# Turning gathered expert rows on TensorE: operands retyped from float32 to float32r

## The reference, cut to what matters

```python
xb = x_pad[rows]                                  # gather the rows of one expert
h = jax.nn.silu(xb @ w_gate[e]) * (xb @ w_up[e])  # 1024 -> 256
yb = (h @ w_down[e]) * rw[:, None]                # 256 -> 1024
return acc.at[rows].add(yb), None
```

## Time and profile before

| | |
|---|---|
| median of 3 runs | 1641.59 us (1641.39 to 1642.97) |
| profiled execution: span from its first to its last instruction | 1640.5 us (no time of it beside the span is given) |
| PE busy | 1578.0 us, 96% of the span |
| PE weight loads | 1310.0 us, 80% |
| DVE busy | 1182.3 us, 72% |
| ACT busy | 1032.5 us, 63% |
| POOL busy | 503.7 us, 31% |
| mean granted TensorE clock | 0.979 of full speed |

### The profile page before, as it was taken

How to read it: one execution, slowest core, us unless ns; L and a number is a source line. 1 busy time by engine, 2 the same in 40 slices (tenths; PEclk the granted TensorE clock), 3 DMA queues, 4 the chain that set the end, 5 groups by cost and what they waited for, 6 DMA issues and landing times.

```text
span 1640.5 us, 32188 instructions
## 1 busy us (share of the span) xinstructions
PE 1578.0 (96%) x8246; PEld 1310.0 (80%) x8247; DVE 1182.3 (72%) x2036; ACT 1032.5 (63%) x1706; POOL 503.7 (31%) x495
## 2 busy tenths in 40 slices
PE   6999999999999999899999999999999999999986
PEld 6897888888887788778878888888888888888863
DVE  4214777777777788847777787777876787888866
ACT  3214666666666655527677787666776777877854
POOL 0000000000000135432544454543454445454426
PEclk9999999999999999899999999999999999999995
DMA  7223222222123533657999999999999999999987
GB/s 245 91 81 91 72 48 68 58 65 71 45 71 103 170 134 138 227 196 281 337 291 318 305 357 367 326 289 264 334 318 288 274 353 331 342 368 370 367 252 282
DMA packets 161320, 368.63 MB, mean 225 GB/s; under 512 B 53009, under 2 KB 73489, under 8 KB 161265
## 3 DMA queue, kind: packets, MB, share of 16 engines
q1 hardware_dynamic: 136272, 284.21, 49.7%
q0 software_dynamic: 24992, 83.73, 19.7%
HBM read 294.39 MB, written 65.11 MB: 219 GB/s over the span
## 4 chain that ended last, share of the span: by engine, by line
PE 72%; DVE 8%; DMA 8%; issue 5%; ACT 3%; ACTq 2%; POOL 1%; SPq 0%; DVEq 0%; POOLq 0%
PE bank_pair L1025 6%; PE bank_pair L1031 6%; PE bank_pair L1028 6%; DMA sums_scratch<-ys,sidx 5%; PE q_ps L91 4%; PE q_ps L93 4%; PE q_ps L92 4%; PE out_ps L916 4%; PE k_ps L894 4%; PE out_ps L1084 3%; PE out_ps L1085 3%; PE q_ps L1015 3%; PE k_ps L1052 2%; PE k_ps L1053 2%; PE k_ps L1060 2%
## 5 line engine op out<-in xcount | busy, mean ns | idle before, releaser
L1918 DVE TENSOR_TENSOR gu_lo<-raw_gu,gu_hi 128x1024 fp32r<-128x1024 f32 x260 | 306.3, 1220 | 25.5 <-ACT gu_hi L1396 25.5
L1396 ACT CAST gu_hi<-raw_gu 128x1024 fp32r<-128x1024 f32 x260 | 253.2, 1050 | 2.3 <-DMA raw_gu<-in_moe_w_gate_dram 1.5
L1025 PE MATMUL bank_pair<-gu_hi,xb_hi 128*128 128x512 f32 x576 | 233.1, 405 | 5.5 <-DVE gu_lo L1918 4.2
L1028 PE MATMUL bank_pair<-gu_lo,xb_hi 128*128 128x512 f32 x576 | 226.9, 394 | 0.0
L682 POOL DMA_INDIRECT sums_scratch<-ys,sidx x63 | 122.1, 1939 | 148.9 <-DMA sums_scratch<-ys,sidx 116.0
L1918 DVE TENSOR_TENSOR dn_lo<-raw_dn,dn_hi 128x1024 fp32r<-128x1024 f32 x130 | 152.6, 1213 | 2.9 <-ACT dn_hi L1396 2.4
L1031 PE MATMUL bank_pair<-gu_hi,xb_lo 128*128 128x512 f32 x576 | 142.7, 390 | 2.0 <-DVE xb_lo L1922 2.0
L1301 ACT CAST pt_hi<-k_ps 128x512 fp32r<-128x512 f32 (+1 forms) x192 | 85.7, 482 | 75.4 <-PE k_ps L894 74.7
L1025 PEld LDWEIGHTS bank_pair<-gu_hi,xb_hi 128*128 128x128 f32 x576 | 110.1, 191 | 28.8 <-issue 6.4
L613 POOL IOTA e<- 128x64 f32 x1 | 0.2, 185 | 428.8 <-DVE xs L1714 428.8
L1396 ACT CAST dn_hi<-raw_dn 128x1024 fp32r<-128x1024 f32 x130 | 130.0, 1052 | 2.9 <-DMA raw_dn<-in_moe_w_down_dram 2.9
(11 more groups left out here) (306 smaller groups left out, 3973.7 us busy)
## 6 DMA issues: line engine op xcount, KB each, us to landing
raw_gu<-in_moe_w_gate_dram SPq DMA_DIRECT2D x128, 512.0 KB, 6.8
raw_gu<-in_moe_w_up_dram SPq DMA_DIRECT2D x128, 512.0 KB, 8.6
raw_dn<-in_moe_w_down_dram SPq DMA_DIRECT2D x128, 512.0 KB, 8.3
wqk<-in_fox_w_in_dram SPq DMA_DIRECT2D x66, 128.0 KB, 2.5
v_scratch<-v_out SPq DMA_DIRECT2D x32, 256.0 KB, 2.8
va<-v_scratch SPq DMA_DIRECT2D x16, 512.0 KB, 4.7
fin<-sums_scratch SPq DMA_DIRECT2D x16, 512.0 KB, 8.3
xs<-in_x_dram SPq DMA_DIRECT2D x8, 512.0 KB, 7.4
```

The lines of the kernel that those rows point to most:

```text
L1025: i = pe.matmul(o3, xb_hi[s][:, c], g_hi[:, :, c], start=c == 0, stop=False, skip_group_check=True)
L1028: pe.matmul(o3, xb_hi[s][:, c], g_lo[:, :, c], start=False, stop=False, skip_group_check=True)
L1396: a.copy(hi, raw).then_inc(S[done], 1)
L1918: dve.tensor_tensor(lo, raw, hi, ALU.subtract).then_inc(S[lo_ok], 1)
```

## The change

A second identity `identr` of type F32R is allocated (128x128, 512 bytes in each partition, ahead of all later buffers) and filled by POOL with a copy of `ident`, after the two masks. POOL and PE each get one more wait for this copy. The 8 transposes of `turn_rows` and the 8 of `turn_further` read the rows as F32R (a reinterpretation of the same bytes, with no rounding ahead of it), take `identr` as moving operand and write PSUM as F32R. The other transposes of the kernel (L794, L894, L901, L983, L1039, L1093) stay as they were.

```diff
         ident = sb("ident", [P, P])
         identb = sb("identb", [P, P], BF16)
+        identr = sb("identr", [P, P], F32R)
...
             g.affine_select(out=upto[:], in_=upto[:], compare_op=ALU.is_ge, fill=0.0, base=0,
                             pattern=[[1, T]], channel_multiplier=-1).then_inc(S["masks"], 1)
+            g.tensor_copy(identr[:], ident[:]).then_inc(S["masks"], 1)
+
+            pool.wait_ge(S["masks"], 8)
             pool.wait_ge(S["v_ps"], NVC * TT // 2)
...
             def turn_rows(src, ps):
                 v = strided(src[:, 0:D])
                 for c in range(DC):
-                    i = pe.transpose(ps[:, c * P:(c + 1) * P], v[:, c], ident[:])
+                    i = pe.transpose(ps[:, c * P:(c + 1) * P].bitcast(F32R), v[:, c].bitcast(F32R), identr[:])
                 return i
...
                 v = strided(xg[2][rows, 0:D])
                 for c in range(DC):
-                    i = pe.transpose(banks[1][:, FF + c * XR:FF + (c + 1) * XR], v[:, c], ident[rows, rows])
+                    i = pe.transpose(banks[1][:, FF + c * XR:FF + (c + 1) * XR].bitcast(F32R), v[:, c].bitcast(F32R), identr[rows, rows])
                 i.then_inc(S["x_turned"], 1)
...
+            pe.wait_ge(S["masks"], 8)
             pe.wait_ge(rows_in[0], 16)
             pe.wait_ge(S["r1_ok"], TT - 1)
             turn_rows(xg[0], q_ps).then_inc(S["turned"], 1)
```

## The result

The changed kernel takes 1651.07 us (median of 4 runs, 1649.98 to 1652.06) against 1642.28 us for the kernel before (median of 4, 1641.39 to 1643.32). The ratio is 1.0055 with an interval of 1.0042 to 1.0069: 9.0 us slower, interval 6.9 to 11.3. 1641.3 was forecast and 1645.5 was the upper end, so it is more than the range held.

The account below looks back on a forecast made before the run. PE's instruction stream in the experts was taken to bound the kernel. Span 1640.5 + 0 (loads) - 0.3 (group ends) + 0 (copy) + 0 (memory) = 1640.2, with 1.1 around it 1641.3 us; range 1635 to 1645.5.

Parts of the forecast that it names:

- The load of the rows: PE's weight loads in 824 turns: rounded strided pitch 112 ns against 111, +0.8 us, taken as 0 +-2.5 us.
- rival 2: Loads in both kinds of turn: stride and type surcharges add up, pitch 161 ns, +41 us, 1683 us; chance 0.06.
- The bounds: Rounded strided load in a turn: from 51 ns less (plain adjacent load) to about 50 ns more (stride on top of type).
- Wrong towards slower: loads of 240: Sign in the turns' weight loads: a duration of 240 ns would show the forecast wrong towards slower.
- Right: loads of 190: Sign in the first-row turns: loads still at some 190 ns, eight of them in 0.97 us, would show the forecast right.
- The ends of a group: Behind each group's last turn: `q_ps` finished about 49 ns earlier, taken as -0.3 us, bounds 0 and -3.5 us.
- The stream goes from 109 to about 60: Moving identity in first-row turns: rounded stream about 60 ns instead of 109, alone moving no start as the load takes 111.
- copy, wait and memory: Identity's POOL copy and PE's wait: cost 0, without cover 0.3 us; buffers shifted by 512 bytes: unpriced, +-1 us.
- Rule and row on the fast load: Turn loads: the skill's rule read literally makes F32R loads fast; rows say otherwise, bf16 load 97 ns, rounded 188.

Follow-up runs that it names:

- e7: Kernel before with first-row turns as ordinary rounded products with the identity, adjacent columns (low bits lost, wrong weight rows), further rows plain: 1641.51 us, one run.
- e6: Kernel before with first-row turns as ordinary rounded products with the rounded identity, same stride (low bits lost), further turns plain: 1703.71 us, ratio 1.0373.
- e4: Kernel before with first rows turned rounded from adjacent columns (wrong weight rows), further rows plain and strided: 1631.39 us, ratio 0.9929.
- e5: Kernel before with first rows turned plain from adjacent columns (wrong weight rows), further rows plain and strided: 1639.41 us, ratio 0.9989.
- b9: Kernel before with rows written in turn order by the normalisation, all turns adjacent, down weights reordered, only first rows rounded: 1627.16 us, ratio 0.9907.
- e1: Changed kernel with both kinds of turn back to plain, keeping `identr`, its copy and the waits: 1641.94 us, ratio 1.0001 to the kernel before.
- e11: Kernel before with only the further rows rounded, from adjacent columns (wrong weight rows), first rows plain and strided: 1634.91 us, one run.
- b5: Kernel before with gate and up weights loaded in adjacent-column order (1 KB runs), both kinds of turn adjacent, first rows rounded: 1642.09 us, ratio 1.0006.

## Why the prediction was wrong, step by step

- **The step that failed** is "The load of the rows", the term 824 x (112 - 111) = +0.8 us, taken as 0 +-2.5. The load's pitch is 133 and 131, so the term is 824 x 0.022 = +18 us nominally, +15.1 between the neighbouring matmuls. Both neighbours that I set around it were far in the respect that mattered: the earlier trace rows is rounded and adjacent but no turn (e7: 112, e6: 239), is a turn but plain. The agreement of 188 and 193 ns in the earlier trace rows, on which I leaned against rival 2, meant nothing for a turn: a rounded load with adjacent columns lasts 141 ns there (e4), not 188.
- **The bounds held, the spread did not.** +-50 ns contained +22. I then gave +50 a chance of 0.06 and nothing in between any. Between ends so far apart, with no row of the same kind inside, the range should have reached much further up: half of the upper bound alone is 824 x 0.025 = 21 us.
- **Rival 2 had the sign and the sum's form** (surcharges of stride and type add up), and its point of decision, 4 ns per load, was passed by far. Its size was 50 where 22 came: I took the type's surcharge from 142 to 188 ns of *duration*. Durations of loads do not give the pitch: 189 ns belongs to a pitch of 133 in the kernel after and to 112 in the earlier trace rows.
- **So my test for it failed too.** "Wrong towards slower: loads of 240" did not come, and "Right: loads of 190" did, in a kernel that was 9 us slower. Only the other half of it, eight loads in 0.97 us, was a good test: it became 1.12.
- **"The ends of a group"**: the rounded stream does end sooner, but the load binds, so everything behind it comes later. ACT's wait for `q_ps` rose by 4.6 us where 2.3 less was forecast, and in e4, with the load out of the way, it fell from 26.3 to 13.4. The matmul's duration rose to 293, where 225 was forecast. The mechanism was right and its condition was not met.
- **"The stream goes from 109 to about 60"**: e4 and e5, 86 against 109, show that the rounding does remove the stream's limit. The 60 itself lies under the load's 86. In the kernel after it shows once a group: where the turns come behind a wide matmul (41 of 72 groups), the second turn starts 60 ns behind the first, where it was 108 to 109 before; from the third on the loads set the pace.
- **Right:** PE's stream in the experts decides; the load sets the pitch before (the 32-wide turns fall from 108 to 62 ns when only the stride goes, b9); copy, wait and memory cost 0 within 2 us (e1); the clock stayed at 1.00; the rounded rows did not load faster than the plain ones. The Trainium skill (TensorE: Matmul & The Clock Gate, LDWEIGHTS) gives a rule by columns and not by rows; an estimate from that page is 128 / 1.2 = 107 ns for a load of 128 columns. The plain strided turn (108 to 112) and the adjacent ordinary product (112) agree, and so does that 32 rows take no less than 128; the 62, 86, 133 and 239 do not, and there the measurement decides.
- **Rule and row on the fast load:** plain float32 turns with adjacent columns load with a pitch of 62 ns. The Trainium skill (TensorE: Matmul & The Clock Gate, Weight-path perf modes) excludes FP32 from fast loads; whatever makes these quick, in this case the plain type is the quicker of the two four-byte ones in a turn.
- **What reaches the result:** +15.1 us on PE gave +9.0, -14.2 gave about -12 (e4, by its ratio), e6's some +67 gave +61. In the change, 3.9 us are idle time that PE no longer has. The remaining 2 or so were not located and lie within the scatter of single profiles: from the first to the last turn of first rows it is 901.2 us before, 913.3 after, and 904.2 in e1, whose turns are those of before.

**Open:** what inside the chip takes the 22 ns. It comes with every rounded turn and not with its stride, width, bank, neighbours or memory, and it is there where only the loads set the pitch (e11). Whether the load itself takes it, or a step between the load and its matmul, is not shown: the loads do not last longer (193 to 189 ns, 136 to 133). Rows, identity and result were always retyped together, so which of the three brings it wasn't tested either. Rounded turns of the attention's probabilities, whose columns are adjacent already, were not tried.

## What to carry to other kernels

Before you make a matmul's stream quicker, find out whether its weight load binds: read the pitch of the loads (eight of them in one row of the timeline), not their duration, and look for a narrow twin. A turn of four-byte data wants adjacent columns. With them the rounded type pays where 128 columns stream through (109 to 86 ns) and costs where only 32 do (62 to 84); with a stride it costs in both (111 to 133, 108 to 131). When the order has to change somewhere, change it where a few instructions off the critical path write the data once, rather than in the transfers of the weights.

## What the runs showed of the hardware

- The rounded type makes the loads in turns start 21 to 24 ns further apart for 128 columns: 62 to 83-86 adjacent, 108 to 131 and 111 to 133 strided.
- The same stride costs some 50 ns in a turn of either type, but 127 ns in an ordinary rounded product (112 to 239).
- A 32-wide plain turn with adjacent columns goes at 62 ns, where every eighth column took 108.
- Weights transferred in runs of 1 KB instead of 4 KB undid a gain of 17 us on PE (b5), although their bytes are the same; with runs of 4 KB 24.5 us on PE gave 15.0 (b9).
- A stride of 512 bytes in the write (DVE) or the read (ACT) of 128x1024 float32 made the instruction 1.6 and 2.0 times as long: 1285 to 2083 ns, 1059 to 2069.
